# Order of four small steps in a decoder-trunk kernel: two value transposes and the gates' transpose moved into the attention loop, two small products one piece later, one weight split sooner

## The chip, the core and the metric

The kernel runs on one core of a Trainium2 chip. The metric is the device time of one execution in microseconds (us), as the median of several runs. TensorE is called PE, its weight loads PEld, VectorE DVE, ScalarE ACT, GpSimd POOL and SyncE SP.

## What is computed

One step of a two-layer decoder trunk over 288 tokens: 256 of a prompt and 8 requests with 4 new tokens each. All weights and activations are float32. Cut to what matters here, each layer is:

```
h = rms_norm(x) @ w_in                       # one wide projection, split by columns
o_a = dilated attention, three patterns      # 8 heads, prompt and samples
o_b = b * conv3(c * h)                       # gated short convolution
kc, vc = compress(k_cmp, v_cmp)              # silu(blocks @ w1) @ w2, keys then rotated
o_c = sigmoid gates g_c * (compressed, selected, window attention)
m = sum over branches of sigmoid(g_merge) * ((o * silu(z)) @ w_up)
x = x + m @ w_out                            # after the last layer: rms_norm
```

For the samples, the raw rows that are compressed and the selected keys and values lie in pages of a pool in memory and are fetched page by page through a page table.

## The kernel before

**One list of steps.** Python builds one list, `program_steps()`, with `steps(layer)` for each of the two layers. Each engine's program walks this same list and emits its own share of each step. So the place of a step in the list sets its place in the queues of PE, ACT, DVE and POOL alike; engines meet only at semaphores. SP has an order of its own, over the list `loads`, and waits for the steps that free its buffers.

**Precise products.** Each large matrix product is made of three products of rounded float32: the weights are split in four quarters, each rounded by ACT (`round`, line 1540) to a high part and subtracted by DVE (`split`, line 1782) to a low part. `precise` at line 1027 then does 24 matmuls of 288 columns for a 128-wide tile (three for each of 8 slices of the depth).

**Banks in rings.** PSUM's eight banks are four rings of two: PJ (projections), TR (transposes), SC (scores), O (outputs). A step may write its bank only when the step two places back in the same ring has been released by the engine that reads it. The order of steps therefore says which step waits for which.

- TR before, around the change: `vturn 1`, `vturn 2`, `vturn 3`, `vturn 0`, `gct`, then two banks for each `pturn` of a mixer A unit. The second bank of `pturn 0` waits for `gct` to be released.
- PJ before: `gc`, `feat za0`, `gates`, `feat za1`, `feat za2`, ...

**Steps that move.** After the 28 projection tiles come `vturn 1`, `vturn 2` (transposes of values to token rows, line 1040; ACT copies each with a factor, line 1508), `gc` (the gates' columns, line 1104; ACT copies it, line 1549), `vturn 3` (values of new tokens, ACT line 1511) and `vturn 0` (values of the selected branch, ACT line 1500). `gct` turns the gates' sums to token rows (line 1113; ACT applies tanh, line 1553; DVE line 1791). `gates` spreads the gates to the samples' rows (line 1228; DVE lines 2022 to 2028).

**The attention loop** has 16 units `i` (branch, half of the prompt, head). A turn of it is:

```
out.append(("score", u))
out += ahead("round") + ... + ahead("split") + ...
out += [("exp", u)] + next_feat() + second("round") + late + [("scale", u)] + second("split")
... ("pv", units[i - 2]) ...
out += blocks.get((i, 0), [])
if i >= 1: out.append(("pturn", units[i - 1]))
if i % 2: out += next_feat()
out += blocks.get((i, 1), [])
```

`score` is 24 small matmuls on PE (line 1157) and a masked maximum on DVE (line 1722); `exp` is on ACT (1581), `scale` on DVE (1932), `pturn` on PE (1040) with copies by ACT (1591), and `feat` is a tile of 24 matmuls (1027) with tanh on ACT (1566) and a product on DVE (1889).

**The samples' stage.** `piece()` is one sixteenth of the hidden layer of the compression: `hid` (24 matmuls, line 1275), for every second one `hpost` (DVE 1985, 1987) and `htail` (ACT tanh 1628, DVE 1997), and in between the rounding and splitting of the page piece two ahead (`pround` ACT 1623, `psplit` DVE 1974). `kc hb` makes compressed keys (PE 1282, ACT copy 1632, DVE rotation 2009 to 2017), `vc hb` compressed values (PE 1290, ACT copy 1642). `sscore`, `sexp`, `sturn`, `spv` are scores, softmax, transposes and weighted values of the samples (PE 1309 and 1336; ACT 1670; PE 1040; PE 1377, 1387, 1405). `imp` and `impsum` rank the blocks (PE 1347, 1353; DVE 2062 to 2074).

**SP's pages.** SP issues the selected keys' pages (line 851) only after the load of the second window block, which waits for `spv 0 win`. After the last of these issues it waits for the scores `sscore 0 slc1`, loads half of the first gate's weights (line 942), and then the pages of values. The `round` of the first gate waits for that half.

Of the kernel before, what the change touches and what calls it, by code (L numbers as in the profile page):

```python
# [201 lines left out]
def prompt_units():  # L202
    return [(br, qt, r) for br in "AC" for qt in range(2) for r in range(REP)]
# [29 lines left out]
def steps(layer):  # L233

    out = []
    def splits(item, *quarters):


        return [(kind, item, q) for q in quarters for kind in ("round", "split")]
# [8 lines left out]
    for i in range(len(TILES)):  # L248
# [20 lines left out]
            out.append(("rope",) + ROPE_AT[i])  # L269
        if i == TILES.index(("cmp", 1)):  # L270
            out.append(("pairs",))
    out += [("vturn", 1), ("vturn", 2), ("gc",), ("vturn", 3), ("vturn", 0)]
    units, feats, late = prompt_units(), list(FEATS), []

    def next_feat():

        n = len(FEATS) - len(feats)
        return [("feat",) + feats.pop(0)] + ([("pages", 0)] if n == 20 else [("pages", 1), ("pages", 2)] if n == 23 else [])
# [3 lines left out]
    def ahead(kind):  # L282

        return [(kind, ("feat", n // 4), n % 4) for n in itertools.islice(coming[kind], 1)]
# [2 lines left out]
    begun = iter(pieces)  # L287
    begin = lambda: [(kind,) + z for z in itertools.islice(begun, 1) for kind in ("pround", "psplit")]
    w1_split = lambda kind, part: [("wround", kind, part), ("wsplit", kind, part)]
    blocks = {(0, 1): [("gates",)], (4, 1): [("vstack",)], (10, 0): [("ghid",)],  # L290
              (11, 0): [("ghidt",)], (12, 0): [("gkc",)], (13, 0): [("cscore", 0)], (14, 0): [("cturn", 0)],
              (14, 1): [("cpv", 0), ("gateC", 0)], (15, 0): [("cscore", 1)] + begin(), (15, 1): begin()}
    for i, u in enumerate(units):
        out.append(("score", u))
        if i == 0:
            out.append(("gct",))
        second = (lambda kind: ahead(kind)) if i % 2 else (lambda kind: [])
        out += ahead("round") + ([("gkcr",)] if i == 13 else []) + ahead("split") +             {13: w1_split(0, 0), 15: w1_split(0, 1)}.get(i, [])
        out += [("exp", u)] + next_feat() + second("round") + late + [("scale", u)] + second("split")
        late = []  # L300
        if i >= 2:
            out.append(("pv", units[i - 2]))
            if units[i - 2][0] == "A" and units[i - 2][2] == REP - 1:
                late = [("gateA", units[i - 2][1])]
        out += blocks.get((i, 0), [])
        if i >= 1:
            out.append(("pturn", units[i - 1]))
        if i % 2:
            out += next_feat()
        out += blocks.get((i, 1), [])  # L310
# [3 lines left out]
    def piece(*between):  # L314

        z = next(done)
        ends = z[3] and z[0:3] != (1, 1, 1)
        return [("hid",) + z, *between] + [("hpost",) + z[0:3]] * ends + begin() + [("htail",) + z[0:3]] * ends
# [8 lines left out]
           piece(("spv", 0, "anew"), ("soA", 0)) + piece(("sscore", 0, "cmp"), ("sexp", 0, "cmp")) + \  # L327
           [("sgateA", 0), ("sscore", 1, "d4")] + piece(("cmpt", 0), ("sscore", 1, "mix"), ("sturn", 0, "win")) + \
           [("sexp", 1, "A")] + piece() + \
           [("vc", 0), ("spv", 0, "win"), ("sturn", 1, "d4")] + piece() + \  # L330
           [("spv", 1, "d4"), ("sturn", 1, "mix"), ("imp", 0)] + piece() + \
           [("impsum", 0), ("spv", 1, "mix"), ("sturn", 1, "anew")] + \
           piece(("spv", 1, "anew"), ("soA", 1)) + piece() + [("kc", 1)] + \
           piece(("sgateA", 1), ("sscore", 1, "win")) + piece() + \
           [("sscore", 1, "cmp"), ("sexp", 1, "cmp"), ("sscore", 0, "slc0"), ("sscore", 0, "slc1"), ("sexp", 0, "slc")] + piece()
    out += [("cmpt", 1), ("sturn", 0, "cnew"), ("sscore", 1, "new"), ("hpost", 1, 1, 1), ("htail", 1, 1, 1), ("sturn", 0, "slc0"), ("sexp", 1, "win"),
            ("imp", 1), ("spv", 0, "cnew"), ("sturn", 0, "slc1"), ("vc", 1), ("impsum", 1)] + splits(("gate", 0, 0), 0) + \
           [("sscore", 1, "slc0"), ("sscore", 1, "slc1")] + splits(("gate", 0, 0), 1) + [("sturn", 1, "win"), ("sexp", 1, "slc")] + \
           [("gate", 0, 0, 0), ("spv", 1, "win")] + splits(("gate", 0, 0), 2) + \
           [("gate", 0, 0, 1), ("spv", 0, "slc0"), ("spv", 0, "slc1"), ("sturn", 1, "cnew"), ("soC", 0)] + splits(("gate", 0, 0), 3) + \  # L340
# [29 lines left out]
def program_steps():  # L370

    halves = lambda layer, q: [(layer, (kind, ("tok", 0), q)) for kind in ("round", "split")]
    starts = [start(0, i) for i in range(KT)]
    out = sum(starts[0:2], []) + [(0, ("firsthalf",))] + sum(starts[2:4], []) + halves(0, 0) + sum(starts[4:], []) + [(0, ("square", 0))] + halves(0, 1)
    out += [(0, ("square", 1)), (0, ("square", 2)), (0, ("round", ("tok", 0), 2))]
    for layer in range(DEPTH):
        out += steps(layer)
        for i in range(KT):
            early = {i: [(layer, (kind, ("down", 1), i - 1)) for kind in ("round", "split")] for i in range(1, 5)}
            if layer + 1 < DEPTH:  # L380
                early |= {5: halves(layer + 1, 0), 6: halves(layer + 1, 1), 7: [(layer + 1, ("round", ("tok", 0), 2))]}
            out += early.get(i, [])[0:1] + [(layer, ("down", i // 4, i % 4))]
            out += start(layer + 1, i)[::-1 if layer + 1 == DEPTH else 1] + early.get(i, [])[1:2]
    return out + [(DEPTH, ("root",)), (DEPTH, ("spread",))] + [(DEPTH, ("y", i)) for i in range(KT // 2)]
# [1986 lines left out]
```

How the kernel before makes its waits and increments, by code:

```python
def wait(eng, sem_value):  # L189
    if sem_value[1] > 0:
        eng.wait_ge(*sem_value)
# [638 lines left out]
    def page_numbers(queue, z):  # L830
        queue.wait_ge(late_in, 16 * len(LATE))
        return [{i: queue.value_load(page_no[0:1, hb * RB * PAGES + i:hb * RB * PAGES + i + 1], min_val=0,
                                     max_val=NPH - 1) for h in range(2) for i in page_share(("cmp", 1 - z, hb, h), z)}
                for hb in range(HB)]
# [1 line left out]
    def load_pages(queue, key, z, numbers):  # L837
        kind, which, hb, h = key
        if kind == "cmp" and hb == 0:
            queue.wait_ge(*big_used(Now.layer, split_keys[which - 2]))
        elif key[0:3] == ("slc", 0, 1):
            queue.wait_ge(*big_used(Now.layer, ("kA", 1)))
        elif key[0:3] == ("slc", 1, 1):
            queue.wait_ge(*PJ.is_full(("hid", 1, h, 1)))
        else:
            queue.wait_ge(*pages_used(*PG[z].before(key)))
        for i in page_share(key, z):
            b, g = divmod(i, PAGES)
            src = a["pool"][Now.layer, bass.ds(numbers[hb][i], 1), :, which + 2 * (kind == "slc"), :]
            queue.dma_start(pgb(key)[:, b, g, :], src.rearrange("a p n -> (a p) n")).then_inc(*PG[z].fill(key))
# [3 lines left out]
        @block.sync  # L855
# [14 lines left out]
            load_x(0)
            load_first_half(0, first_of_all_in)
            load_x(1)
            load_first_half(1, first_in[0])
            sp.wait_ge(x_in[0], 16)
            load_x(2)
            load_x(3)
            load_first(1)
            sp.wait_ge(x_in[2], 16)
            load_first(2)
```

## Time and profile before

| | |
|---|---|
| median of 3 runs | 927.91 us (927.34 to 931.07) |
| profiled execution, its time | 928.51 us |
| its span on the core | 926.8 us |
| PE busy | 904.8 us, 98% |
| DVE, ACT, POOL busy | 647.7, 453.4, 189.2 us |

The span is the profiled time without what lies around it (1.7 us). The busy time of an engine is the union of its instructions. The two layers show the same stages: the first from about 20 to 346 us, the second from about 474 to 800 us.

### The profile page before, as it was taken

How to read it: one execution, taken by the hardware profiler on the slowest of the kernel's cores; microseconds unless marked ns; L12 is line 12 of the kernel's file. 1: busy time of each engine (PE TensorE's matmuls, PEld its weight loads, DVE VectorE, ACT ScalarE, POOL GpSimd, SP SyncE). 2: the span in 40 equal slices, each digit the busy share in tenths (PEclk: the TensorE clock that was granted, in tenths of full speed). 3: DMA queues.
4: the chain of work that ended last, by engine and by line, in shares of the span. 5: the costliest groups of instructions: out<-in, count | busy, mean ns of one | idle time of the engine just before them, and what ended most of it. 6: DMA issues, size and time to landing. Idle time of an engine off the chain costs nothing.

```text
span 926.8 us, 21926 instructions
## 1 busy us (share of the span) xinstructions
PE 904.8 (98%) x8176; PEld 846.9 (91%) x8176; DVE 647.7 (70%) x1447; ACT 453.4 (49%) x896; POOL 189.2 (20%) x321
## 2 busy tenths in 40 slices
PE   6999999999999999999999999999999999999997
PEld 6999899988888799999999998999888878999996
DVE  6999767677666467656769996666766565775574
ACT  6444655564543454344543447654554444443352
POOL 1200000237658300000000000003574771000000
PEclk9999999999999999999999999999999999999998
DMA  9762985736979874333665577666469799335421
GB/s 327 290 225 104 423 335 205 271 118 217 306 224 299 255 319 161 138 138 120 256 254 206 196 301 267 257 271 271 165 194 301 239 272 332 159 140 196 165 92 51
DMA packets 66345, 209.89 MB, mean 226 GB/s; under 512 B 12192, under 2 KB 49776, under 8 KB 56256
## 3 DMA queue, kind: packets, MB, share of 16 engines
q1 hardware_dynamic: 57200, 187.67, 55.3%
q0 software_dynamic: 8896, 20.82, 7.1%
q8 instruction: 65, 1.06, 0.5%
q14 instruction: 40, 0.33, 0.1%
q10 hardware_dynamic: 144, 0.01, 0.0%
HBM read 202.48 MB, written 41.36 MB: 263 GB/s over the span
## 4 chain that ended last, share of the span: by engine, by line
PE 86%; SPq 4%; DMA 3%; ACT 2%; DVE 2%; issue 2%; DVEq 0%; ACTq 0%
PE bank L1027 63%; PE bank L1275 7%; PE bank L1040 4%; SPq L851 4%; PE bank L1195 2%; DMA paged<-in_pool 2%; PE bank L1165 1%; PE bank L1157 1%; PE bank L1309 1%; ACT paged_r L1540 1%; DMA x<-in_x 1%; PE bank L1405 1%; PE bank L1208 1%; PE bank L1377 1%; ACT kvp L1508 0%
## 5 line engine op out<-in xcount | busy, mean ns | idle before, releaser
L1782 DVE TENSOR_TENSOR big_r<-big,paged_r 128x1024 fp32r<-128x1024 f32 (+1 forms) x160 | 194.6, 1221 | 74.0 <-ACT paged_r L1540 73.1
L1027 PE MATMUL bank<-xnT_high_r,paged_r 128*128 128x288 f32 x768 | 231.7, 302 | 0.0
L1027 PE MATMUL bank<-xnT_r,paged_r 128*128 128x288 f32 x704 | 207.6, 295 | 0.0
L1027 PE MATMUL bank<-xnT_high_r,big_r 128*128 128x288 f32 x704 | 207.1, 294 | 0.0
L1540 ACT ACTIVATE paged_r<-big 128x1024 fp32r<-128x1024 f32 (+1 forms) x160 | 166.7, 1049 | 4.3 <-DMA big<-in_w_feat 2.4
L1027 PE MATMUL bank<-short_r,big_r 128*128 128x288 f32 x568 | 167.5, 295 | 0.0
L1027 PEld LDWEIGHTS bank<-xnT_high_r,paged_r 128*128 128x128 f32 x768 | 144.0, 188 | 5.1 <-issue 2.7
L1027 PEld LDWEIGHTS bank<-xnT_high_r,big_r 128*128 128x128 f32 x704 | 132.4, 188 | 0.0
L1027 PEld LDWEIGHTS bank<-xnT_r,paged_r 128*128 128x128 f32 x704 | 132.2, 188 | 0.0
L1027 PE MATMUL bank<-short_r,paged_r 128*128 128x288 f32 x440 | 130.9, 298 | 1.2 <-DVE big_r L1782 1.1
L1027 PE MATMUL bank<-kvp_r,paged_r 128*128 128x288 f32 x440 | 130.4, 296 | 0.0
L1027 PEld LDWEIGHTS bank<-short_r,big_r 128*128 128x128 f32 x568 | 106.6, 188 | 0.0
L851 POOL DMA_DIRECT2D paged<-in_pool x166 | 88.7, 536 | 47.8 <-PE bank L1275 32.4
L1003 POOL TENSOR_SCALAR short<-short,small 128x128 f32<-128x128 f32 (+1 forms) x64 | 53.8, 856 | 182.5 <-DVE small L1940 182.5
L1027 PEld LDWEIGHTS bank<-short_r,paged_r 128*128 128x128 f32 x440 | 82.6, 188 | 2.2 <-DVE big_r L1782 1.3
L1678 ACT ACTIVATE tanh<-bank 128x288 f32<-128x288 f32 x48 | 19.7, 410 | 129.5 <-PE bank L1027 129.5
L1027 PEld LDWEIGHTS bank<-kvp_r,paged_r 128*128 128x128 f32 x440 | 82.9, 188 | 0.1
L1722 DVE CUSTOM_DVE_ANT_0 short<-bank,masks 128x384 f32<-128x384 f32 (+4 forms) x120 | 45.7, 424 | 30.8 <-PE bank L1157 13.3
L1581 ACT ACTIVATE short<-short,small 128x384 f32<-128x384 f32 (+2 forms) x96 | 47.5, 496 | 16.7 <-DVE small L1922 16.7
L1027 PE MATMUL bank<-long_r,paged_r 128*128 128x288 f32 x224 | 47.8, 295 | 0.0
L1040 PE MATMUL bank<-ident,short 128*128 128x128 f32 (+3 forms) x290 | 44.3, 279 | 0.4 <-ACT PT L1649 0.3
L1040 PEld LDWEIGHTS bank<-ident,short 128*128 128x128 f32 (+3 forms) x290 | 31.5, 140 | 7.4 <-issue 4.5
(347 smaller groups left out, 1818.9 us busy)
## 6 DMA issues: line engine op xcount, KB each, us to landing
big<-in_w_tok SPq DMA_DIRECT2D x13, 2048.0 KB, 9.9
big<-in_w_feat SPq DMA_DIRECT2D x12, 2048.0 KB, 8.2
big<-in_w_gate SPq DMA_DIRECT2D x10, 2048.0 KB, 9.6
out_kept_dil<-in_cache_dil SPq DMA_DIRECT2D x16, 1020.0 KB, 13.2
paged<-in_pool SPq DMA_DIRECT2D x218, 64.0 KB, 4.5
big<-in_w_up SPq DMA_DIRECT2D x12, 1024.0 KB, 8.9
paged<-in_pool POOLq DMA_DIRECT2D x166, 64.0 KB, 5.1
big<-in_kv_win SPq DMA_DIRECT2D x4, 2048.0 KB, 8.8
```

Source lines behind the costliest of these rows:

```text
L851: queue.dma_start(pgb(key)[:, b, g, :], src.rearrange("a p n -> (a p) n")).then_inc(*PG[z].fill(key))
L1003: last = nc.gpsimd.tensor_scalar(part, part, rec[slot][:, 2 * z + g:2 * z + g + 1], None, ALU.mult)
L1027: last = mm(out, l, r, start=(c == 0 and i == 0), stop=(c == n - 1 and i == 2))
L1040: last = nc.tensor.transpose(out, in_, ident[0:n, 0:n])
L1157: last = mm(sc(s + (g,))[CLASS * h:CLASS * (h + 1), cols], qTA[rows, t, r, mine], kT[rows, t, mine if t else slice(0, SEQ)], start=True, s ...
L1195: last = mm(ob(okey)[HD * g:HD * (g + 1), P * r:P * (r + 1)], v_prompt[:, kb, VCOL[t] + HD * g:VCOL[t] + HD * (g + 1)], PTp[:, P * (KV * i ...
L1275: last = mm(out, w, r[:, :, j, :], start=(lh == 0 and j == 0 and part == 1 and n == 0), stop=(lh == 1 and j == 3 and n == 2), skip_group_c ...
L1540: f(high_part(item, q)[:, rest], split_part(bigb(item), item, q)[:, rest], ACT.Copy)\
L1581: last = f(part, part, ACT.Exp, bias=nmx[slot][:, c:c + 1], accum_out=den[slot][:, c:c + 1])
L1678: f(tanh[:, tanh_slot[s], :], pj(s)[:, 0:T], ACT.Tanh, scale=0.5).then_inc(*PJ.release(s))
L1722: return v.tensor_tensor_reduce(out, scores, mask, 1.0, -3e38, ALU.add, ALU.max, top)
L1782: v.tensor_tensor(l_part[:, rest], full[:, rest], h_part[:, rest].bitcast(FP32), ALU.subtract)\
```

## The change

`vturn 3` and `gct` go to the end of the loop's turn 0, behind its `feat`; `vturn 0` goes into turn 1, between `scale` and `pturn 0`; `gates` goes from the end of turn 0 to the end of turn 1. `vc 0` goes from before `spv 0 win` to behind the piece that follows it. `kc 1` goes from before a piece to the middle of it, between `sgateA 1` and `sscore 1 win`. The round and split of the first quarter of the first gate's weights go from behind `impsum 1` to before `spv 0 cnew`. No instruction is added or removed.

```diff
-    out += [("vturn", 1), ("vturn", 2), ("gc",), ("vturn", 3), ("vturn", 0)]
+    out += [("vturn", 1), ("vturn", 2), ("gc",)]
...
-    blocks = {(0, 1): [("gates",)], (4, 1): [("vstack",)], (10, 0): [("ghid",)],
+    blocks = {(0, 0): [("vturn", 3), ("gct",)], (1, 0): [("vturn", 0)], (1, 1): [("gates",)], (4, 1): [("vstack",)], (10, 0): [("ghid",)],
...
     for i, u in enumerate(units):
         out.append(("score", u))
-        if i == 0:
-            out.append(("gct",))
...
-           [("vc", 0), ("spv", 0, "win"), ("sturn", 1, "d4")] + piece() + \
-           [("spv", 1, "d4"), ("sturn", 1, "mix"), ("imp", 0)] + piece() + \
+           [("spv", 0, "win"), ("sturn", 1, "d4")] + piece() + \
+           [("vc", 0), ("spv", 1, "d4"), ("sturn", 1, "mix"), ("imp", 0)] + piece() + \
            [("impsum", 0), ("spv", 1, "mix"), ("sturn", 1, "anew")] + \
-           piece(("spv", 1, "anew"), ("soA", 1)) + piece() + [("kc", 1)] + \
-           piece(("sgateA", 1), ("sscore", 1, "win")) + piece() + \
+           piece(("spv", 1, "anew"), ("soA", 1)) + piece() + \
+           piece(("sgateA", 1), ("kc", 1), ("sscore", 1, "win")) + piece() + \
...
-            ("imp", 1), ("spv", 0, "cnew"), ("sturn", 0, "slc1"), ("vc", 1), ("impsum", 1)] + splits(("gate", 0, 0), 0) + \
+            ("imp", 1)] + splits(("gate", 0, 0), 0) + [("spv", 0, "cnew"), ("sturn", 0, "slc1"), ("vc", 1), ("impsum", 1)] + \
```

## Rows read from the trace of the kernel before

**Rows 1.** The page, part 1: busy us, share of the span, instructions.

```profile
PE 904.8 (98%) x8176; PEld 846.9 (91%) x8176; DVE 647.7 (70%) x1447; ACT 453.4 (49%) x896; POOL 189.2 (20%) x321
```

**Rows 2.** Waits of PE: line waited for; us, times, longest.

```profile
PE bank L1040 <- ACT kvp L1508: 2.0, 4, 0.6
PE bank L1282 <- DVE kvp L1997: 1.5, 2, 0.8
...
PE bank L1027 <- DVE paged_r L1782: 0.7, 2, 0.4
...
PE bank L1405 <- DMA paged<-in_pool: 0.7, 2, 0.5
...
PE bank L1336 <- DMA paged<-in_pool: 0.2, 1, 0.2
```

**Rows 3.** Timeline of PE, layer 0: start, us, line, tiles, idle before.

```profile
104.58 0.60 PE L1040 MATMUL bank<-ident,oT_c 128*32 128x128 f32 x4 [0.59 <-ACT kvp L1508]
...
106.06 0.89 PE L1157 MATMUL bank<-kT,long 64*64 64x256 f32 x24
106.89 0.80 PE L1113 MATMUL bank<-group_sum,short 128*128 128x24 f32 x6
...
111.00 0.62 PE L1228 MATMUL bank<-gct,pick 32*128 32x24 f32 x4
111.56 0.89 PE L1157 MATMUL bank<-kT,long 64*64 64x256 f32 x24
...
115.67 0.82 PE L1040 MATMUL bank<-ident,short 128*128 128x128 f32 x6
```

**Rows 4.** Timeline of ACT in the same stretch.

```profile
105.59 0.66 ACT L1511 ACTIVATE kvp<-bank,small 32x512 f32<-32x512 f32 x1
106.17 0.86 ACT L1500 ACTIVATE kvp<-bank,small 128x128 f32<-128x128 f32 x3
107.05 1.28 ACT L1553 ACT_TABLE_LOAD   x1
108.34 0.60 ACT L1553 ACTIVATE gct<-bank,small 128x24 f32<-128x24 f32 x3
...
114.96 0.62 ACT L1581 ACTIVATE short<-short,small 128x384 f32<-128x384 f32 x1 [2.49 <-DVE small L1922]
...
116.46 1.05 ACT L1540 ACTIVATE paged_r<-big 128x1024 fp32r<-128x1024 f32 x1
117.41 0.85 ACT L1591 ACTIVATE PT<-bank 128x512 f32<-128x512 f32 x2
```

**Rows 5.** Timeline of DVE in the same stretch.

```profile
111.63 0.45 DVE L1889 SCALAR_TENSOR_TENSOR oT_a<-tanh,bank 128x288 f32<-128x288 f32 x1
...
112.86 0.27 DVE L2022 TENSOR_TENSOR sgt<-bank,row_head 128x24 f32<-128x24 f32 x2
...
113.61 0.56 DVE L1722 CUSTOM_DVE_ANT_0 short<-bank,masks 128x384 f32<-128x384 f32 x1
...
114.83 1.22 DVE L1782 TENSOR_TENSOR big_r<-big,paged_r 128x1024 fp32r<-128x1024 f32 x1
```

**Rows 6.** Timeline around `vc 0`: PE, then ACT's read of the exp's sum.

```profile
273.97 1.15 PE L1290 MATMUL bank<-w,kvp 128*64 128x64 f32 x16 [0.32 <-DVE kvp L1997]
275.04 1.08 PE L1387 MATMUL bank<-big,PT 128*32 128x128 f32 x32
...
275.04 0.19 ACT L1670 ACTIVATION_READ_ACCUMULATOR short<-short,small 128x1 f32 x1
```

**Rows 7.** Timeline around `kc 1`: DVE, and PE at the end of a piece.

```profile
293.92 0.44 DVE L2009 STREAM_SHUFFLE kT<-kT 128x256 f32<-128x256 f32 x1
...
295.93 0.28 PE L1040 MATMUL bank<-ident,o_sb 128*128 128x128 f32 x1
...
300.62 0.22 DVE L1722 CUSTOM_DVE_ANT_0 short<-bank,masks 128x63 f32<-128x63 f32 x1 [0.21 <-PE bank L1309]
```

**Rows 8.** Landing of the first gate's first half (line 942).

```profile
DMA to landing us min/median/max: 5.8/6.6/7.4
```

## The prediction

> **What bounds the kernel now.** I read the page first: PE is busy 904.8 of 926.8 us [rows 1]; the engines behind it have room, DVE least. No instruction is added or removed, so the change can only give back idle time of PE, or make new. All of that idle time is 22 us. Next I read the waits of PE, for this is the account from which the change can draw. Four kinds of wait belong to the moved steps: 2.0 us in four waits of transposes for ACT's value copies, 1.5 us in two waits of `kc 1`, 0.7 us in two waits of the first gate for its split [rows 2], and 0.32 us of `vc 0` in each layer [rows 6]. Together 4.8 us, 0.5% of the time, if all went and nothing came in their place. The last view is the timeline of PE, ACT and DVE around each moved step, to see what is late next [rows 3 to 7]. The two layers repeat each other, so I work each part for one layer and double it.
>
> **Part 1: the transposes and `gct` go into the loop.** Removed: `vturn 3` waits 0.59 us [rows 3] and `vturn 0` the rest of 1.0 us per layer [rows 2] for ACT, which is still copying `vturn 1` and `vturn 2`. But the ring of transposes has two banks. Before, the second bank of `pturn 0` waited for `gct`, long released. After, the order is `vturn 3`, `gct`, `vturn 0`, `pturn 0` first and second bank, so the second bank waits for ACT to copy `vturn 0`. That copy now stands in ACT's queue behind `exp` 1, the tanh of `feat za1` and a round of 0.95 us, while PE makes `vturn 0` right behind `za1`. Is ACT in time? Both sides, each step by the distance between row starts:
>
> PE [rows 3]: `gc` ends at 104.58 − 0.59 = 103.99. Score 0 takes 0.83 (106.06 to 106.89), `gct` with `feat za0` 4.11 (106.89 to 111.00), score 1 with `feat za1` 4.11 (111.56 to 115.67), `vturn 3` and `vturn 0` 1.05 (104.58 to 106.06 less the second wait), and the first four of `pturn 0`'s six transposes about 0.4, an estimate from their row: 114.5. `za0` ends at about 108.2 and `za1` at 113.6 in this sum.
>
> ACT and DVE [rows 4, 5]: ACT has copied `gc` at 105.59. A round takes 0.95 (116.46 to 117.41) and brings 106.5, the table load (1.29) 107.8, `exp` 0 with the tanh of `za0` 1.5 us (114.96 to 116.46) 109.3; `za0` is ready for it by then. DVE then takes 0.2 to start and 1.23 for the product and `scale` 0 (110.8), 0.2 for `gct`, and 1.22 (113.61 to 114.83) for the maxima of score 1 (112.2). ACT's `exp` 1 ends at 113.5, its tanh waits for `za1` (113.7) and ends at 114.0, the round at 115.0, and the copies of `vturn 0` (0.88, 106.17 to 107.05) at 115.9. PE stood ready at 114.5: it waits 1.4 us.
>
> The edges: the stall is 0 if ACT should be 1.4 us further ahead than I have it; it is 1.8 us if ACT keeps the lag of before, where it left that round 1.74 us after PE had ended `za1` (117.41 against 115.67), plus 0.88 of copies less the 0.85 PE spends on transposes. I take 1.4, for `gates` (0.75 us of DVE, 112.86 to 113.61) leaves the way to the maxima. Part 1 is then −1.0 + 1.4 = +0.4 us per layer, between −1.0 and +0.8. `gates` itself costs the same on PE in its new place, and its bank is long free. The two stores of values that POOL issues behind `vturn 0` start later, but what asks for them is `ghidt`, ten turns on, and POOL has nothing else queued until then.
>
> ACT's table load is one row of 1.28 us, and the next ACTIVATE starts 1.29 us after it [rows 4]. The Trainium skill, in "ScalarE: Activation LUTs", section "What ACT_TABLE_LOAD costs", adds a drain of about 1.38 us to each switch of set, so some 2.66 us in all. Here the trace differs: no such gap stands behind the load. By the page the stall of part 1 would be longer by up to 1.4 us per layer (an estimate from it); I go by the row.
>
> **Part 2: `vc 0` one piece later.** Removed: its wait of 0.32 us [rows 6]. But in its place comes `spv 0 win` (1.0 us, its row less the overlap) and then `sturn 1 d4`, which needs ACT's `exp`, and this ends at about 275.25 (275.04 + 0.19) whatever PE does, since it hangs on DVE work that does not move. PE gets to `spv` at 273.97 − 0.32 = 273.65 and to `sturn` at 274.65, and stands 0.6 us. Before, `vc 0` with its 1.07 us (273.97 to 275.04) was the cover. So part 2 is −0.32 + 0.6 = +0.3 us per layer; bounds 0 and +0.4, because the end of the `exp` is a row. In the new place `vc 0` has its inputs long ready, and ACT's copy of it stands behind one tanh and has the time of `spv 1 d4` and a transpose step before the next piece asks for the bank, so I cost it at nothing; without that cover it would be up to 0.5 us.
>
> It has a second effect: `spv 0 win` ends 1.4 us sooner, and SP's run of page issues starts that much sooner. In layer 0 PE waits 0.2 us for the last of these pages [rows 2]; that wait goes.
>
> **Part 3: `kc 1` into the next piece.** Removed: 0.75 us of waiting for DVE [rows 2]. Moved: `kc`'s rotation on DVE, four operations of which the first is 0.44 us [rows 7], so 1.7 us, with the wait for PE's `kc` and ACT's copy in front, about 0.6 us (an estimate). It now stands before the maxima of `sscore 1 win`, `hpost`, `psplit` and `htail`, and all these before the maximum of `sscore 1 cmp`. Before, that one was taken at 300.62, 4.7 us behind the piece's end at 295.93, and DVE had stood 0.2 us just before it. After, the 2.3 us of rotation and its wait come in front, less some 0.9 us in which DVE had stood for `sgateA` and the window scores (an estimate), so DVE gets to the maximum about 6.1 us behind the piece's end and releases the bank at 6.35. PE, which now does `kc` (0.6 us) in this stretch, wants that bank for `sscore 0 slc1` at 6.0. So a new wait of 0.3 to 0.4 us comes. Part 3 is −0.75 + 0.35 = −0.4 us per layer; bounds −0.75 and 0. The softmax of the selected scores is later by about 1.2 us too, but a whole piece of PE's work stands between it and its transposes, so I cost that at nothing; without this cover it would be those 1.2 us.
>
> **Part 4: the first gate's split sooner.** It would save its wait of 0.35 us [rows 2]. But between that gate and the weighted values stands another clock: SP starts the page loads of the values when `sscore 0 slc1` is full, and at their end PE waits for DMA 0.5 us in layer 0 and 0.2 in layer 1 [rows 2]. These loads do not start sooner relative to PE, so what PE gains before that point it gives back there: 0. Bounds: −0.35 (pages land sooner) and +0.4 (below). The round now stands in ACT's queue ahead of two copies and so asks for its half of the gate's weights about 0.9 us sooner; the landing took 5.8 us in one layer and 7.4 in the other [rows 8]. ACT may thus stand some tenths in the slower of them, with the copies of `sturn` and `vc 1` behind it; two transposes' and one score's time on PE cover about 0.8 us of that, and what goes past shows.
>
> **The sum.** Layer 0: +0.4 + 0.3 − 0.4 − 0.2 = +0.1; layer 1: +0.4 + 0.3 − 0.4 = +0.3. In all +0.4 us on the profiled 928.5. The median of the runs shown lies 0.6 us below the profiled execution, so I forecast 928.3 us: no change. What a measurement of this kernel can tell from no change is about 0.5%, 4.6 us.
>
> **The rivals.**
>
> *The waits go and stay gone.* ACT keeps up with `pturn 0`, and DVE with the compressed scores. For it: ACT is busy only 49% [rows 1]. Against it: the two queues worked out above. It gives −1.0 − 0.75 per layer, with `vc 0` between −0.32 and +0.3, and −0.2 once: −3.1 to −4.3 us, so about 924.3.
>
> *The gate's gain is kept.* Pages land sooner, as SP's whole run begins 1.4 us sooner and meets less traffic. It adds −0.35 to −0.5 per layer to the forecast: 927.5. Against it: that SP waits for `sscore 0 slc1` in between.
>
> *Slower: ACT is the bound of turns 0 and 1.* The table load now sits before `exp` 0 instead of behind the last copies. If the first function being exp brings a set without tanh, a second load of 1.29 us stands before the tanh of `za0`, on the path to the maxima and so to `vturn 0`'s copy, and the stall grows from 1.4 to 2.7 us in each layer: +2.6 us to the forecast, 930.9. It decides from two loads per turn 0 instead of one. Against it: before, one load serves both functions.
>
> *Slower by DMA.* The same traffic at other times makes one late page: the two waits at the values' pages grow from 0.5 to 1.5 us, +2: 930.
>
> **How the numbers follow.** Forecast 0.52; waits stay gone 0.22; gate's gain kept 0.10; second table load 0.04; DMA or a stall larger than worked out 0.12. The range, 924.6 to 930.8, reaches into the first rival on one side and to the last two on the other, and leaves about 0.15 out. Faster by over 0.5% needs nearly every wait gone at once: 0.05. Slower by over 0.5% needs two of the slow cases together: 0.04. Within 0.5%: 0.91.
>
> **What the next profile would show.** Right: the waits of L1040 for L1508 are gone and one of about 1.4 us stands at the second transposes of `pturn 0`, for ACT L1500; a wait of 0.6 us at `sturn 1 d4` for ACT L1670; none at L1282 and L1290; 0.3 to 0.4 at L1336 for DVE's maximum L1722; the gate's wait for L1782 gone and the one of L1405 for DMA longer by as much. Wrong: no wait at `pturn 0` (then faster by up to 2.8 us), or page loads that end earlier or later relative to `sscore 0 slc1` than before.

## The result, and the profile after

The changed kernel takes 933.5 us (median of 10 runs, 928.54 to 934.62), the kernel before 928.19 (10 runs, 927.2 to 931.07). The ratio is 1.0049, with a 95% interval of 1.0032 to 1.0066: slower by some 4.5 us, which is what the means of the ten runs differ by (the medians by 5.3). I had forecast 928.3 and a range up to 930.8. Line numbers of the changed kernel are 2 lower than before: L1498, L1538 and L1668 are what L1500, L1540 and L1670 were.

The page, parts 1 and 2 (busy us; the granted clock in 40 slices):

```profile
PE 906.3 (97%) x8176; PEld 849.1 (91%) x8176; DVE 648.4 (70%) x1447; ACT 453.6 (49%) x896; POOL 188.6 (20%) x321
...
PEclk9999989999999999999999999999999999999998
```

The span is 931.2 us against 926.8, and PE is busy 1.5 us longer than in [rows 1] with the same 8176 instructions: part of the loss is not waiting, it is slower work. One slice of the clock shows an 8, the one around 116 to 140 us. The waits of PE, answering to [rows 2]:

```profile
PE bank L1038 <- ACT kvp L1498: 5.9, 2, 4.1
...
PE bank L1038 <- ACT short L1668: 1.2, 2, 0.6
...
PE bank L1273 <- DVE paged_r L1972: 1.1, 2, 0.5
PE bank L1334 <- DVE small L1720: 0.7, 2, 0.4
```

All waits of [rows 2] are gone, those for DMA too. In their place stand the three that I had worked out (the second bank of `pturn 0`, `sturn 1 d4`, the compressed scores' maximum) and one that I had not (L1273, a page split). The first of them was to be 1.4 us in each layer; it is 4.12 in layer 0 and 1.74 in layer 1.

To read where time came from I take the start of the same matmul in both traces. First layer 0 of before, then after (start us, us):

```profile
102.82 0.45 PE L1104 MATMUL bank<-x,w_gc 128*32 128x288 f32 x4
...
119.61 0.45 PE L1157 MATMUL bank<-kT,long 64*64 64x256 f32 x4
...
280.94 0.26 PE L1347 MATMUL bank<-overlap,PTc 128*128 128x17 f32 x1
...
306.84 0.29 PE L1347 MATMUL bank<-overlap,PTc 128*128 128x17 f32 x2
...
321.98 0.32 PE L1405 MATMUL bank<-paged,PT 128*32 128x128 f32 x4 [0.52 <-DMA paged<-in_pool]
```

```profile
103.01 0.45 PE L1102 MATMUL bank<-x,w_gc 128*32 128x288 f32 x4
...
125.03 0.45 PE L1155 MATMUL bank<-kT,long 64*64 64x256 f32 x4
...
286.67 0.29 PE L1345 MATMUL bank<-overlap,PTc 128*128 128x17 f32 x2
...
312.32 0.29 PE L1345 MATMUL bank<-overlap,PTc 128*128 128x17 f32 x2
...
326.24 0.43 PE L1403 MATMUL bank<-paged,PT 128*32 128x128 f32 x8
```

The five are `gc`, score 2, `imp 0`, `imp 1` and the first weighted values of the selected pages. The shifts are +0.19, +5.42, +5.73, +5.48 and +4.26; each part of the change lies between two of them. The same five in layer 1 stand at +4.28, +4.67, +4.98, +5.24 and +4.52. The differences are what each part does:

| stretch | part | forecast per layer | layer 0 | layer 1 |
|---|---|---|---|---|
| `gc` to score 2 | 1 | +0.4 | +5.23 | +0.39 |
| to `imp 0` | 2 | +0.3 | +0.31 | +0.31 |
| to `imp 1` | 3 | −0.4 | −0.25 | +0.26 |
| to the values | 4 | 0 | −1.22 | −0.72 |

Nearly all of the loss is part 1 in layer 0; layer 1 does what was forecast. Here is that place, PE around `pturn 0` first (start us, us, idle before), then ACT:

```profile
113.42 0.49 PE L1038 MATMUL bank<-ident,prod 128*128 128x128 f32 x3
113.91 0.66 PE L1038 MATMUL bank<-ident,short 128*128 128x128 f32 x4
118.69 0.69 PE L1038 MATMUL bank<-ident,short 128*128 128x128 f32 x2 [4.12 <-ACT kvp L1498]
```

```profile
105.50 0.47 ACT L1547 ACTIVATE short<-bank 128x288 f32<-128x288 f32 x1
108.10 1.06 ACT L1538 ACTIVATE paged_r<-big 128x1024 fp32r<-128x1024 f32 x1 [2.13 <-DMA big<-in_w_feat]
109.18 1.28 ACT L1579 ACT_TABLE_LOAD   x1
110.47 0.62 ACT L1579 ACTIVATE short<-short,small 128x384 f32<-128x384 f32 x1
...
115.34 0.61 ACT L1579 ACTIVATE short<-short,small 128x384 f32<-128x384 f32 x1 [1.25 <-DVE small L1920]
...
116.84 1.04 ACT L1538 ACTIVATE paged_r<-big 128x1024 fp32r<-128x1024 f32 x1
117.79 0.84 ACT L1498 ACTIVATE kvp<-bank,small 128x128 f32<-128x128 f32 x3
```

PE is ready at 114.57 (118.69 less 4.12), as worked out (114.5). ACT is not: the round in front of the table load waits 2.13 us for the second feature group's weights. What follows, down to the copy of `vturn 0`, keeps the order of the forecast; the copies of `vturn 3`, of `gct` and one more round fit into ACT's idle time before `exp` 1. The copy of `vturn 0` comes 2.7 us later than worked out (118.6 against 115.9); 2.13 of that is the load. In layer 1 the round waits for no load. And the stand has a consequence. The windows around it (PE, PEld, DVE, ACT, POOL busy; the granted clock; DMA share; GB/s):

```profile
114.00:118.60 4.60, 0.57 (x4) 0.33 (x4) 3.84 (x11) 3.35 (x11) 0.00 (x0) 0.81 1.09 442
118.60:119.10 0.50, 0.41 (x3) 0.42 (x3) 0.50 (x1) 0.50 (x2) 0.00 (x0) 0.50 0.64 261
119.10:123.70 4.60, 4.60 (x21) 4.60 (x20) 0.40 (x1) 0.39 (x2) 1.04 (x2) 0.50 0.73 251
123.70:130.00 6.30, 6.30 (x74) 5.72 (x73) 3.50 (x12) 3.08 (x7) 0.00 (x0) 1.00 0.05 20
```

From 118.69 to 123.7 PE works at a granted clock of 0.50, which is 1.2 of 2.4 GHz, after having stood. The matmuls of the projection show it:

```profile
119.89 0.44 PE L1025 MATMUL bank<-xnT_high_r,paged_r 128*128 128x288 f32 x1
120.13 0.44 PE L1025 MATMUL bank<-xnT_r,paged_r 128*128 128x288 f32 x1
```

They start 0.24 us apart, and the same two 0.13 apart at full clock. What the half clock costs as a whole, layer 1 tells, in which PE does the same steps at full clock:

```profile
574.37 0.44 PE L1038 MATMUL bank<-ident,short 128*128 128x128 f32 x2 [1.74 <-ACT kvp L1498]
578.47 0.89 PE L1155 MATMUL bank<-kT,long 64*64 64x256 f32 x24
```

From the second bank of `pturn 0` to score 2 it needs 4.10 us there and 6.34 in layer 0 (118.69 to 125.03): 2.24 us for the clock. The late load shows at one more place. In layer 0 the first bank of `pturn 0` starts at 113.91, just behind the end of `scale` 0 on DVE, which hangs on `exp` 0 and so on the round; from `gc` to the begin of the stand PE takes 0.23 us longer than in layer 1 (11.56 against 11.33).

```profile
113.11 0.75 DVE L1930 TENSOR_SCALAR short<-short,small 128x384 f32<-128x384 f32 x2
```

So the sum for layer 0 closes with each term read from rows: part 1 without its stand is −1.35 (layer 1: +0.39 − 1.74), plus 0.23, plus 4.12 of stand, plus 2.24 for the clock: +5.24, for the +5.23 of the table. The Trainium skill puts the penalty of the gate at the throttled time times one less the granted share ("TensorE: Matmul & The Clock Gate", section "Terms"). Over the 5.0 us in which PE worked at half clock that makes 2.5, and the trace has 2.24; over the whole fall of 6.8 us (from 116.9, of which PE stood the first 1.8) it makes 3.4, and the trace does not agree.

### The profile page after: what moved, and what is told of

Its sections match the earlier page's. It is cut to its first block, busy times and chain, and to the rows that moved or that the text cites. A ratio compares the mean times of both kernels' runs of the same rounds, so it can differ in the third digit from the quotient of the medians.

```text
span 931.2 us, 21924 instructions
## 1 busy us (share of the span) xinstructions
PE 906.3 (97%) x8176; PEld 849.1 (91%) x8176; DVE 648.4 (70%) x1447; ACT 453.6 (49%) x896; POOL 188.6 (20%) x321
## 4 chain that ended last, share of the span: by engine, by line
PE 83%; DVE 4%; ACT 4%; issue 3%; DMA 3%; SPq 2%; DVEq 0%; ACTq 0%
PE bank L1025 58%; PE bank L1273 8%; PE bank L1038 4%; PE bank L1193 2%; SPq L831 2%; DMA big<-in_w_feat 2%; PE bank L1163 1%; PE bank L1307 1%; ACT paged_r L1538 1%; PE bank L1155 1%; PE bank L1403 1%; PE bank L1206 1%; PE bank L1375 1%; DMA big<-in_w_tok 1%; PE bank L1334 1%
## 5 line engine op out<-in xcount | busy, mean ns | idle before, releaser
L1538 ACT ACTIVATE paged_r<-big 128x1024 fp32r<-128x1024 f32 (+1 forms) x160 | 166.7, 1049 | 5.9 <-DMA big<-in_w_feat 4.4
L1579 ACT ACTIVATE short<-short,small 128x384 f32<-128x384 f32 (+2 forms) x96 | 47.6, 496 | 14.9 <-DVE small L1920 14.8
```

Of the source, the lines that this page charges most:

```text
L1538: f(high_part(item, q)[:, rest], split_part(bigb(item), item, q)[:, rest], ACT.Copy)\
L1579: last = f(part, part, ACT.Exp, bias=nmx[slot][:, c:c + 1], accum_out=den[slot][:, c:c + 1])
```

## The experiments

### Which part costs

**Part 1 alone** (e1), on the kernel before:

```diff
-    out += [("vturn", 1), ("vturn", 2), ("gc",), ("vturn", 3), ("vturn", 0)]
+    out += [("vturn", 1), ("vturn", 2), ("gc",)]
...
-    blocks = {(0, 1): [("gates",)], (4, 1): [("vstack",)], ...
+    blocks = {(0, 0): [("vturn", 3), ("gct",)], (1, 0): [("vturn", 0)], (1, 1): [("gates",)], (4, 1): [("vstack",)], ...
...
-        if i == 0:
-            out.append(("gct",))
```

> Only the two value transposes, the gates' transpose and `gates` stand in the loop; the other three moves are undone. Theory 1 (late weights and clock): in layer 0 the first round of the second feature group waits about 2 us for its load, the stall at the second bank of `pturn 0` is about 4 us, and PE then runs some 4.7 us at half clock, +5.2 us in layer 0 and +0.4 in layer 1: 5.5 us over the kernel before. Theory 2 (the bank order alone): the same sign, but the loss is there without any wait for a load. Theory 3 (the page traffic of the other moves): no loss here, within 1 us of the kernel before.

Measured: 932.06 us (5 runs) against 928.62 (22), ratio 1.004 [1.0026, 1.0053]. The loss is there; it is 3.4 us and not the 5.5 expected, with the late load, the stand and the fall of the clock all smaller:

```profile
106.97 1.06 ACT L1538 ACTIVATE paged_r<-big 128x1024 fp32r<-128x1024 f32 x1 [1.24 <-DMA big<-in_w_feat]
```

```profile
117.56 0.44 PE L1038 MATMUL bank<-ident,short 128*128 128x128 f32 x2 [3.46 <-ACT kvp L1498]
```

The round waits 0.9 us less for its load than with the whole change, and the stand is 0.7 us shorter; the half clock follows it here too, for 3.4 us in the place of 6.8, and costs 1.5.

**Parts 2, 3 and 4 alone** (e2, the changed kernel with part 1 undone):

> Only the moves of `vc 0`, `kc 1` and of the first gate's split; the transposes stand as before. Theories 1 and 2: from the trace of the changed kernel +0.3 for `vc 0`, -0.25 and +0.26 for `kc 1` and -1.2 and -0.7 for the gate's part with the pages, in all -1.3 us against the kernel before. Theory 3: about +5 us.

Measured: 927.71 us (11 runs), ratio 0.9994 [0.9985, 1.0003]. By the same marks as in the table its parts are, in layers 0 and 1, +0.32 and +0.32, −0.22 and +0.25, −1.22 and −0.41. So the loss is part 1's. The other three gain 0.9 us by the medians, and their interval reaches from a gain of 1.4 to a loss of 0.3.

### What makes the stand of part 1 longer than worked out

SP issues the load of the second feature group at 91.46, between copies of the caches. The landings of that load (line 942 after, 944 before, the stretch 90 to 100 us), after and then before:

```profile
who waited for it (us, times):
  ACT paged_r L1538: 2.1, 1
busy tenths in 40 slices 0000000000000000000000000000000000000000
DMA to landing us min/median/max: 16.6/16.6/16.6
```

```profile
DMA to landing us min/median/max: 14.8/14.8/14.8
```

If the load is the cause, putting those copies behind it must shorten the stand (e3, on the changed kernel):

```diff
-                        for _ in range(3 if kind == "feat" else 2):
+                        for _ in range({("feat", 0): 0, ("feat", 1): 6}.get(key, 3 if kind == "feat" else 2)):
```

> The changed kernel, but SP issues the three cache copies of the first feature group only behind the load of the second group, so that these 2 MB meet less traffic. Theory 1: ACT's wait for this load is gone, the stall at `pturn 0` is 1.7 us in both layers as it was in layer 1, no stretch at half clock, and the time is 4.3 us below the changed kernel, near 928 to 929. Theory 2: stall about 4 us and half clock in layer 0 remain, time as the changed kernel within 1 us.

Measured: 931.49 us (6 runs), ratio 1.0029 [1.0017, 1.0041]. This load is now issued at 88.99 and lands 12.4 us behind that, at 101.4: it goes out 2.5 us sooner and takes 4.2 us less, and the run doesn't part the two.

```profile
105.35 1.12 ACT L1538 ACTIVATE paged_r<-big 128x1024 fp32r<-128x1024 f32 x1
```

```profile
116.01 0.44 PE L1038 MATMUL bank<-ident,short 128*128 128x128 f32 x2 [2.10 <-ACT kvp L1498]
```

The round no longer waits, and the stand falls from 4.12 to 2.10 us: the load was 2.0 of its 4.1. What is left is 0.36 more than in layer 1; DVE starts the product of `za0` that much later behind its tanh in layer 0, and I don't know for what. The clock falls with the shorter stand as well (0.65 granted from 116.0 to 120.9). From the second bank to score 2 PE takes 5.62 us for the 4.10 at full clock, so the fall costs 1.5; e3 as a whole is 2 us faster than the changed kernel. So neither theory held whole: the load's delay is a cause, and taking it away mends only half; the order of `vturn 0` and `pturn 0` is the other half. **`vturn 0` behind the projection of turn 1** (e4) removes it, since ACT's copy then isn't between PE and the second bank:

```diff
-    blocks = {(0, 0): [("vturn", 3), ("gct",)], (1, 0): [("vturn", 0)], (1, 1): [("gates",)], ...
+    blocks = {(0, 0): [("vturn", 3), ("gct",)], (1, 1): [("vturn", 0), ("gates",)], ...
```

> The changed kernel with one step moved: `vturn 0` stands behind `feat za2` in turn 1 instead of in front of `pturn 0`, so that no bank of `pturn 0` waits for its copy. The load of the second group stays as late as in the changed kernel. Theory 1 and 2 both: no stall at `pturn 0` beyond 0.5 us, full clock, and with the waits of the old place gone -1.0 us per layer and -1.3 for the other parts: about 925 against 928. If the late load alone can stop PE (theory 1 in a strong form, through the exponentials), a stall of about 2 us remains in layer 0 and half clock may follow: 928 or more.

Measured: 925.99 us (11 runs), ratio 0.9971 [0.9962, 0.998]: faster than before.

```profile
114.09 0.82 PE L1038 MATMUL bank<-ident,short 128*128 128x128 f32 x6
```

All six transposes of `pturn 0` run in one group with no wait, at full clock. Part 1 in this form gives −1.56 us in each layer. So the idea of part 1 is good, and one step's place was wrong.

In this trace, though, the load landed 14.6 us behind its issue and the round waited only 0.2 us for it. What this order does with a late load, a later run shows by chance: e10, described below, has the same order, and its load landed 16.5 us behind its issue (L1547 and L1045 are its round and its transposes):

```profile
107.92 1.06 ACT L1547 ACTIVATE paged_r<-big 128x1024 fp32r<-128x1024 f32 x1 [2.14 <-DMA big<-in_w_feat]
```

```profile
113.73 0.87 PE L1045 MATMUL bank<-ident,short 128*128 128x128 f32 x6 [0.33 <-DVE short L1946]
```

The round waits 2.14 us, as in the changed kernel, and PE stands 0.33 us here and 0.54 at `vturn 0`; from `gc` to score 2 it needs 1.3 us more than in e4, and the clock stays up. In the changed kernel the same lateness came to a stand of 4.12 us and the fall behind it. It is the order that makes a late load dear.

### The other parts

**The gate's split alone** (e5), on the kernel before:

```diff
-             ("imp", 1), ("spv", 0, "cnew"), ("sturn", 0, "slc1"), ("vc", 1), ("impsum", 1)] + splits(("gate", 0, 0), 0) + \
+             ("imp", 1)] + splits(("gate", 0, 0), 0) + [("spv", 0, "cnew"), ("sturn", 0, "slc1"), ("vc", 1), ("impsum", 1)] + \
```

> Only the first gate's split stands sooner; all else as before. The prediction's step (absorbed): the gate's wait of 0.35 us goes and PE's wait for the pages of values grows by as much (0.5 to 0.85 in layer 0, 0.2 to 0.5 in layer 1): no change, within 0.3 us of the kernel before. Rival (kept): both waits are gone, as in the changed kernel, -1.2 us.

Measured: 928.33 us (11 runs) against 928.86 (19), ratio 0.9995 [0.9986, 1.0004]. In its trace PE goes from `imp 1` to the values 1.22 us sooner in layer 0 and 0.83 in layer 1, the same as part 4 in the whole change in layer 0. The gate's wait and the wait for the pages are both gone. By the median of the runs the gain is smaller, 0.5 us, with an interval from a gain of 1.3 to a loss of 0.4. The two waits are not equally sure. The gate's wait (0.40 and 0.34) stands in every trace with the split in its old place, and from `imp 1` to the gate e5 is 0.64 and 0.58 us shorter. The wait for the pages comes and goes: with the split in its old place it is 0.52 and 0.17 us in the two layers before, 0 and 0.87 in e1, and 0 and 0 in e12, which is e1's kernel once more. With the split moved it stands in 2 of the 22 layers traced (0.24 in e7, 0.12 in e9), against 3 of 6. So the gate's gain of 0.6 us per layer is shown, and the rest, up to another 0.6, lies in part in the execution. It is the same with the wait of 0.24 us for a page at the compressed scores, which I had given to `vc 0`: it is gone here and in e12 and present in e1, and `vc 0` stands in its old place in all three.

**`kc 1` back** (e6), and **`kc 1` and `vc 0` back** (e7), both on e4:

```diff
-           piece(("spv", 1, "anew"), ("soA", 1)) + piece() + \
-           piece(("sgateA", 1), ("kc", 1), ("sscore", 1, "win")) + piece() + \
+           piece(("spv", 1, "anew"), ("soA", 1)) + piece() + [("kc", 1)] + \
+           piece(("sgateA", 1), ("sscore", 1, "win")) + piece() + \
```

```diff
-           [("spv", 0, "win"), ("sturn", 1, "d4")] + piece() + \
-           [("vc", 0), ("spv", 1, "d4"), ("sturn", 1, "mix"), ("imp", 0)] + piece() + \
+           [("vc", 0), ("spv", 0, "win"), ("sturn", 1, "d4")] + piece() + \
+           [("spv", 1, "d4"), ("sturn", 1, "mix"), ("imp", 0)] + piece() + \
```

> The kernel with `vturn 0` behind the feature tile, and `kc 1` in its old place. Theory from the trace of the changed kernel (the move of `kc 1` is a loss): PE's wait of 0.53 us at the hidden piece for DVE's page split and 0.36 us at the selected scores go, and 0.78 us at `kc 1` comes back: -0.1 us per layer, no difference that can be measured (925.8 against 926.0). Rival (the prediction's step, a gain of 0.4 us per layer): +0.8 us, 926.8.

> The same kernel with `kc 1` and `vc 0` both in their old places, so that of the change only the transposes (with `vturn 0` behind the feature tile) and the gate's split are left. If only PE's own waits count: -0.3 us per layer for `vc 0` against e6, 925.2. Rival (`vc 0` buys time for the pages): SP's page loads start 1.4 us later, and waits for DMA of 0.2 to 0.9 us come back before the selected scores and values in each layer: 926.3 or more.

Measured: 924.81 us (5 runs), 0.9959 [0.9946, 0.9972], and 924.66 (8 runs), 0.9963 [0.9951, 0.9975], against 928.86. The medians of the two don't tell them apart; their traces do. Between `imp 0` and `imp 1` e4 gains 0.22 us in layer 0 and loses 0.23 in layer 1, e6 gains 0.49 and 0.04: `kc 1` in its new place costs 0.27 us per layer. Up to `imp 0`, `vc 0` in its new place costs 0.32 per layer in e6 against 0.0 in e7. Why `kc 1` costs: DVE in the changed kernel, and PE behind it:

```profile
295.40 0.41 DVE L1983 COPY kvp<-bank 128x256 f32<-128x256 f32 x1
295.85 0.61 DVE L1985 SCALAR_TENSOR_TENSOR kvp<-bank,pe_b,kvp 128x128 f32<-128x128 f32 x2
296.38 1.22 DVE L1972 TENSOR_TENSOR paged_r<-paged,tanh_pages 128x1024 fp32r<-128x1024 f32 x1
297.51 0.42 DVE L1995 SCALAR_TENSOR_TENSOR kvp<-kvp 128x256 f32<-128x256 f32 x1
```

```profile
297.74 0.36 PE L1273 MATMUL bank<-tanh_pages,kvp_w 128*128 128x256 f32 x1 [0.53 <-DVE paged_r L1972]
...
307.16 1.07 PE L1334 MATMUL bank<-paged,qblk 128*32 128x512 f32 x8 [0.36 <-DVE small L1720]
```

The DVE steps that belong to `kc 1` now stand in front of the split of the next page, and PE waits 0.53 us for that split; with the 0.36 at the maximum this is 0.89 in the place of the 0.78 removed. That is 0.11 of the 0.27; the rest has no row of a wait.

### What decides whether the clock falls

Stands of 1.74 us brought no fall, those of 2.10 and more did. To look for the edge, e8 takes e4 and adds stands on purpose: before score units 4, 8 and 12 of each layer ACT runs a chain of short copies into an unused tile, and PE waits for the last.

```diff
+STANDS = {(0, 4): 12, (0, 8): 6, (0, 12): 8, (1, 4): 7, (1, 8): 9, (1, 12): 16}
...
+        if (layer, i) in STANDS:
+            out.append(("stand", i))
...
+                elif k == "stand":
+                    pe.wait_ge(stood, stood_after(layer, s))
...
+                elif k == "stand":
+                    done = STEPS[0:STEPS.index(s)]
+                    act.wait_ge(*PJ.is_full([z for z in done if z[0] == "feat"][-1]))
+                    for n in range(STANDS[layer, s[1]]):
+                        if n:
+                            act.wait_ge(stood, stood_after(layer, s) - STANDS[layer, s[1]] + n)
+                        f(unused[:, 4:8], rn_class, ACT.Copy).then_inc(stood, 1)
```

> The kernel with `vturn 0` behind the feature tile, with six stands put in: before units 4, 8 and 12 of each layer PE waits for a chain of 12, 6, 8 (layer 0) and 7, 9, 16 (layer 1) small ACT instructions, which start when PE's last tile is done; nothing else is changed, the output is that of the reference. Theory (a stand of some 2 us or more brings PE's clock down for a few us behind it, at any place): half clock behind the long stands, full clock behind the short ones, with an edge between 1.7 and 2.1 us. Rival (the clock falls only at turn 1 of layer 0, from what PE did before it): full clock behind all six.

Measured: 949.19 us. Some stands brought the fall and some didn't, and not by length. So the same kernel ran again (e9), and one with other lengths (e10), and with them the changed kernel (e11) and part 1 alone (e12) once more:

```diff
-STANDS = {(0, 4): 12, (0, 8): 6, (0, 12): 8, (1, 4): 7, (1, 8): 9, (1, 12): 16}
+STANDS = {(0, 4): 8, (0, 8): 8, (0, 12): 10, (1, 4): 12, (1, 8): 6, (1, 12): 8}
```

> The program of e8 once more. There six stands of TensorE of 1.78 to 3.85 us, made on purpose before three score units of each layer, were followed by a fall of the granted clock to half in four cases (1.78, 1.96, 2.49 and 3.85 us) and by none in two (2.02 and 3.20 us). Theory A, the place and the work around the stand decide (what TensorE did just before and what it does just behind): the same four fall, the same two do not. Theory B, the moment at which the stand begins decides, which differs from one execution to the next: some other set of the six falls, lengths as before; the time moves with the number of falls, by some 1.5 to 2 us for each.

> The same six places with other lengths: about 2.2 to 2.6 us at the first score place of layer 0 (3.20 before), 2.3 and 2.5 at its other two, about 3.2 to 3.5 at the first place of layer 1 (2.02 before), 1.8 at its second and 2.0 at its third. If length decides, only the stand of over 3 us and perhaps those of 2.5 fall, and 1.8 does not. If place decides (theory A), the four places that fell in e8 fall again and the first score place of neither layer falls, at whatever length. If the moment decides (theory B), falls show no order by place or length.

> The changed kernel once more, with its profile. Theory A (the stand of 4.1 us in layer 0 always brings the fall): 934, granted clock 0.992 to 0.993, half clock behind 118.7. Theory B (the moment decides): the stand of about 4 us is there again, and the clock falls or not; without a fall the span is about 929 and the clock 0.997.

> Part 1 alone once more, with its profile. Theory A: a stand of 3.5 us in layer 0 and the fall behind it, clock 0.994, time 932. Theory B: the same stand, with or without a fall; without one about 930 and 0.996 or more.

Measured: 946.4, 948.66, 932.66 and 934.04 us. The stands in us, in bold those with a fall of the granted clock to 0.50 in them or right behind:

| run | layer 0, unit 4 | 8 | 12 | layer 1, unit 4 | 8 | 12 |
|---|---|---|---|---|---|---|
| e8 | 3.20 | **1.78** | **1.96** | 2.02 | **2.49** | **3.85** |
| e9 | **3.20** | 1.78 | 1.96 | 2.02 | **2.49** | **3.85** |
| e10 | **2.25** | **2.25** | **2.43** | **3.20** | 1.78 | 1.96 |

The windows behind the stands of 3.20 and 1.78 us, in e8 and then in e9 (the granted clock is the third number from the end):

```profile
138.00:142.00 4.00, 4.00 (x48) 3.81 (x48) 2.34 (x6) 2.16 (x5) 0.00 (x0) 1.00 0.04 16
169.50:174.00 4.50, 4.50 (x25) 4.38 (x26) 2.86 (x14) 2.64 (x10) 0.00 (x0) 0.63 0.98 404
```

```profile
136.30:140.70 4.40, 4.40 (x39) 4.21 (x40) 2.34 (x6) 2.19 (x5) 0.00 (x0) 0.61 0.04 15
169.30:174.00 4.70, 4.66 (x46) 4.37 (x48) 2.99 (x15) 3.10 (x11) 0.00 (x0) 1.00 0.93 383
```

The same program with the same stands falls at other places in another execution: neither place nor length alone decides, and the moment at which the stand comes has a part (theory B of the expectations). Length still counts. With the stands of `pturn 0` (layer 0: 4.12, 4.01, 3.96, 3.46, 2.10, all with a fall; layer 1: five of about 1.7, none) the count is 2 of 13 for stands up to 2.02 us and 14 of 15 from 2.10 up. Theory A, that the place decides, has fallen, and so has the sharp edge between 1.74 and 2.10 that I had looked for. For the kernel itself e11 gives a stand of 4.01 and e12 one of 3.96, both with a fall, of 3.4 and 6.8 us, which cost 1.5 and 2.2 by the distance from the second bank to score 2 (5.62 and 6.32). Of the changed kernel's ten timed runs nine have a mean granted clock of 0.992 to 0.995 and spans of 928.6 to 933.0 us; one has 0.997, the clock of the kernel before, and a span of 926.9.

## Why the prediction was wrong, point by point

**What failed is part 1's term, in layer 0.** The sum had +0.4 per layer; layer 1 gave +0.39, layer 0 +5.23. Two things were missing. First, the step "A round takes 0.95 and brings 106.5" started the round at 105.59, as soon as ACT had copied `gc`, and took its weights as landed. They were not: before, that load landed 14.8 us behind its issue at 91.35, at 106.15, already 0.6 us too late for that. That row was there to be read; before, it cost nothing because the round stood behind the copies and the table load. In the new order the landing, 16.6 us behind the issue, sets ACT's whole chain. e3 shows it: without the wait the stand is 2.0 us shorter. Second, the sum had no price for what a long stand does to the clock: 2.2 us behind the stand of 4.12. I had bounded the part by −1.0 and +0.8; neither bound held a late load, and "a stall larger than worked out" had 0.12 together with a late page, at 930 us.

**The mechanism of part 1 was right**: the second bank of `pturn 0` waits for ACT's copy of `vturn 0`, as forecast, and the removed waits are gone (the part without its stand is −1.35 where I had −1.0. The rows show the 0.35: a step's first matmul starts before the row ahead of it has ended, unless it waits. From `gc`, `vturn 3` and `vturn 0` to the next step it is 1.17, 0.60 and 0.45 us before, each without its wait, and 1.11, 0.44 and 0.32 after, in layer 1). The stand of layer 1, where no load is late, is 1.74 for my 1.4. The table load takes one row of 1.28 us in turn 0 (109.18), and the next ACTIVATE starts 1.29 us behind it: no second load, which ends that rival, and again no drain behind it.

**Part 2** was right: 0.62 us of wait at `sturn 1 d4` for a forecast 0.6, +0.31 per layer for +0.3. Its second effect was not shown: the page wait of 0.24 us is also gone where `vc 0` didn't move (e5, and e7), so this gain isn't `vc 0`'s.

**Part 3** had the wrong sign: +0.27 per layer (e4 against e6), for −0.4 with a bound at 0. The wait at the maximum came as worked out (0.36 for 0.35). What I missed is the split of the page in between, which I had named in DVE's queue but not asked who waits for it: 0.53 us.

**Part 4** was wrong at the step "what PE gains before that point it gives back there". It kept the gate's gain, which is 0.6 us for a wait of 0.40, and lost the page wait of 0.52 besides: −1.22 in layer 0, −0.72 in layer 1. That was the rival "the gate's gain is kept", with about twice its price; that the price was passed is in part chance, since the page wait of layer 0 is gone in e1 and e12 as well, which leave the split in its old place. Why the pages end last in one execution and not in another I did not test.

**The rivals.** "The waits go and stay gone" (924.3) did not happen here, but e7, with `vturn 0` one projection later, gets 924.66. That the two numbers meet is luck: e7 keeps the waits of `kc 1` (0.77 and 0.79) and `vc 0`, and comes there with −1.56 per layer for part 1, where the rival had −1.0, and with part 4. "Slower by DMA" named the right resource at the wrong place: a late weight load for ACT, not a late page for PE.

**What stays open.** What moves the landing wasn't tried. With the copies where they were it lies between 14.6 and 16.6 us behind the issue in all traces, and part of that is the execution and not the order: in e1 it made ACT wait 1.24 us, in e12, the same kernel, 1.75. And in one of the ten runs the changed kernel needs no more than the one before; whether its stand was shorter or only the fall stayed away, runs without a trace can't say.

## What to carry to other kernels

When a step moves to where an engine gets to it sooner, ask of each of its inputs when it really arrives: a load that landed 0.6 us too late for the new time cost nothing at the old one, and the landing row tells it before the change is made. Sum the engines' queues as chains that end in PE, and look at every step behind an inserted one, not only at the last. Where a sum ends in a stand of PE of 2 us or more, add the half clock that may follow it (1.5 to 2.2 us here); where a wait goes, expect somewhat more than its row; a layout that avoids the stand altogether (here `vturn 0` behind the projection, 0.9971 in the place of 1.0049) is worth more than one that halves it (1.0029).

## What the runs showed of the hardware

PE's granted clock fell to half behind idle stretches as short as 1.78 us, in kernels in which PE is busy 96 to 97% of the span, and stayed up behind one of 3.20 us; the same program does the one and the other. Of stands from 2.10 us up, 14 of 15 brought it. The fall lasted from 3.4 to 6.8 us and cost 1.5 to 2.2 us behind `pturn 0`, and can begin within the stand, as after (from 116.9, the stand being from 114.57 to 118.69). A removed wait gave back more than its row: 0.64 us from `imp 1` to the gate for a wait of 0.40. A weight load of 2 MB issued among copies landed 14.6 to 16.6 us behind its issue, while the median of its kind is 8.0 in the changed kernel; with the copies put behind it, it was 12.4.
